# Turning the feed-forward input before it is normalised, half by half

## The chip, the cores and the metric

One core of a Trainium2 chip runs the kernel. The metric is the device time of one execution in microseconds (us). Each of the core's engines follows its own list of instructions and waits on semaphores: TensorE (PE; its weight loads are a separate row, PEld), VectorE (DVE), ScalarE (ACT), GpSimd (POOL), and SyncE (SP), which here only issues DMAs.

## The reference

Two transformer blocks over 256 tokens of width 1024. The first mixes a gated convolution, a differential attention and a cross attention. The second mixes a stick-breaking attention and a recurrent unit, adds the result to the residual, and ends with a product-key expert layer, which is where the change lies:

```python
x = x + jnp.einsum('bse,ed->bsd', mixed, w_out[l])
h = rms_norm_2(x, norm_ffn[l])          # x * rsqrt(mean(x^2) + eps) * g
# peer_ffn(h):
q = jnp.einsum('td,dhk->thk', xc, w_query)          # 8 heads x 2 sides x 128
s = jnp.einsum('thpk,hpnk->thpn', q, sub_keys)      # 128 keys per side
top_s, top_i = lax.top_k(s, PEER_TOPK)              # 16 of each side, then 16 of 256 sums
act = jax.nn.gelu(jnp.einsum('td,thkd->thk', xc, u))
return jnp.einsum('thk,thkd->td', (g * act), v)
```

For each of 256 tokens and 8 heads 16 experts are chosen out of 16384; each has a row `u` and a row `v` of 1024 numbers, which are gathered from memory.

## The kernel before

Tokens stand in two tiles of 128 (`TT` = 2), channels in eight tiles of 128 (`KT` = 8). A projection is a slot of 512 output columns; its weights come in two pieces of 256 columns. SP loads a piece into one of two raw buffers, ScalarE writes its rounded high part (L694, "hi"), VectorE the rest (L1146, "lo"), and TensorE multiplies in three products, high by high, high by low, low by high (L377). So a piece takes 48 matmuls of 256 columns, a slot 96. SP loads piece p when the low part of piece p - 2 is done; the split buffers rotate over three, so ScalarE's copy for a piece also waits for the products of the piece three back.

Each engine's order is written out by hand. Around the change it is: the sums of squares `mix1` and `mix0` (`mix_sums`, L578), ScalarE's root of them (L885), VectorE's normalisation and split of the mix (L1390 to L1403); the slots `w0` and `w1` (output projection of the second block's mix, tokens on the output partitions), VectorE adding each to the residual `x_res` (L1737, mark `x2`); then

- `inverse_rms("h3")`: squares of token tile 0 on VectorE (L1180), of tile 1 on ScalarE (L709), their sum (L1186), root (L714), reciprocal (L1190);
- `h3` = `x_res` times inverse rms times gain, on VectorE, token-major, four instructions of 512 channels (L1747). The gain `ffn_gain` is a row of 1024 on all partitions and lies in `conv_in`;
- `turn_input("h3")`: sixteen 128 x 128 transposes on TensorE (L405) into two PSUM units, then high part on ScalarE (L737) and low part on VectorE (L1213). Where a gain per channel is given, `turn_input` uses scaled forms of 256 columns (L743 and L1223), as it does for `x`, `mem` and `b2`;
- `pq0` to `pq3`, the query projections (the first piece of `pq1` is `FIRST_UNDER`); ScalarE copies the queries (L907), TensorE multiplies with the keys (`score`, L589), ScalarE copies the scores (L898).

VectorE then chooses head by head (`choose`, L1410 to L1482). Once a head of 16 picks is chosen, POOL issues 16 gathers (L1802), each 128 rows of 8 KB, `u` and `v` together; there are 256 in all, and eight row buffers. Some row buffers lie in space used earlier (`ROW_FREE`): the one in `conv_in` waits for the mark `h3`. For each pick VectorE takes the dot product of `h3` and `u` (L1489), ScalarE the gelu and a scaled identity (L923, L927), and TensorE adds the weighted `v` (L602). The projections `pq2` and `pq3` run in between.

PSUM has three units of 1024 columns and two banks of 512. `units.take` goes round the three unless a place is given; a taker waits for the previous holder's mark of release. Counting the takes, `mix1`'s sums are in unit 2, `mix0`'s in unit 0, `w0` in unit 1 and `w1` in unit 2.

Of the kernel before, what the change touches and what calls it, by code (L numbers as in the profile page):

```python
# [1 line left out]

# [3 lines left out]
P = 128  # L6
# [4 lines left out]
ACT = mybir.ActivationFunctionType  # L11
AX = mybir.AxisListType.X

T = 256
TT = T // P
D = 1024
KT = D // P
# [12 lines left out]
D_SB = SB_HEADS * SB_HEAD_DIM  # L30
D_RG = D - D_SB
RG_TILES = D_RG // P
# [13 lines left out]
           ("diff_subln_g", 1), ("x_qn_g", 2), ("x_kn_g", 2), ("norm_mix_2", KT),  # L46
           ("q_norm_2", 1), ("k_norm_2", 1), ("conv_w_2", RG_TILES * RG_WIDTH),
           ("conv_b_2", RG_TILES), ("rg_b_a_2", RG_TILES), ("rg_b_x_2", RG_TILES),
           ("rg_lambda_2", RG_TILES), ("out_norm_sb_2", D_SB // P), ("out_norm_rg_2", RG_TILES)]
VECTOR_AT = {}  # L50
for _name, _n in VECTORS:
    VECTOR_AT[_name] = (sum(n for _, n in VECTORS[:len(VECTOR_AT)]), _n)
# [3 lines left out]
class Marks:  # L56
# [13 lines left out]
    def mark(self, kind, key=None, *others, by=1):  # L70

        value = self.values[kind] = self.values.get(kind, 0) + by
        for name in (("#" + kind, value), (kind, key), *others):
            self.names[name] = kind, value
        return self.sem(kind), by
# [58 lines left out]
def build(nc, known, x, mem, vectors, w_in, w_conv_proj, w_diff_proj, w_mem_kv, w_x_proj, w_out,  # L134
          w_in_2, rg_w_a, rg_w_x, w_out_2, norm_ffn, w_query, sub_keys_t, experts, out):
    with ExitStack() as ctx:
# [214 lines left out]
        def pe(e):  # L351
# [33 lines left out]
            def project(s, between=(), place=None):  # L385
                units.take(s.name, place)
                for _ in products(s, 0):
                    pass
                for f in between:
                    f()  # L390
                for _ in products(s, 1):
                    pass

            def turn_input(pair, src, scaled, places=(None, None)):
                for half in range(2):
                    name = f"{pair} turn{half}"
                    unit = units.take(name, places[half])
                    for bank in range(2):
                        for wait in W(*(scaled(half)), units.free(name), ("ident", None)):
                            e.wait_ge(*wait)  # L400
                        for j in range(2):
                            k = 4 * half + 2 * bank + j
                            for t in range(TT):
                                to = (2 * bank + j) * T + t * P
                                m = e.transpose(unit[:, to:to + P], src[:, t, k * P:(k + 1) * P],  # L405
                                                ident[:, :])
                        m.then_inc(*mark("turned", (pair, 2 * half + bank)))

            def head_sums(name):
                sq, unit = work.ap(name), units.take(name + " sums")  # L410
# [193 lines left out]
                                 start=first, stop=g == final_pick[t])  # L604
                m.then_inc(*mark("added", g, ("uv free", g)))

            turn_input("x", x_tm, lambda half: (("scaled", "x", half, 0), ("scaled", "x", half, 1)))
            for s in slots[:4]:
                project(s)
            pending = None  # L610
            for n, s in enumerate(attention):
                if s.name == "v0":
                    turn_input("mem", mem_tm,
                               lambda half: (("scaled", "mem", half, 0), ("scaled", "mem", half, 1)))
                project(s)
                if s.name == "m0":
                    diff_values(DIFF_HEADS - 1)
                if pending in HEAD_NORMS:
                    head_sums(pending)
                elif pending:  # L620
                    diff_norm_sums(int(pending[2:]))
                pending = s.name if s.name in HEAD_NORMS else {10: "dn0", 12: "dn1"}.get(n)
                if 0 <= n - 5 < DIFF_HEADS - 1:
                    diff_values(n - 5)
                if 0 <= n - 4 < DIFF_HEADS:
                    diff_turn(n - 4)
                if 0 <= n - 3 < DIFF_HEADS:
                    diff_scores(n - 3)
                if 0 <= n - 13 < X_HEADS:
                    cross_values(n - 13)  # L630
                if 0 <= n - 12 < X_HEADS:
                    cross_turn(n - 12)
                if 0 <= n - 11 < X_HEADS:
                    cross_scores(n - 11)
# [5 lines left out]
            for name in ("xg1", "cg0", "cg1", "dp0", "dp1", "xp0", "xp1", "cp0", "cp1", "o0", "o1"):  # L640
                project(slot[name])

            turn_input("b2", xn, lambda half: (("scaled", "b2", half, 0), ("scaled", "b2", half, 1)))
            project(slot["q2"])
            project(slot["k2"])
            head_sums("q2")
# [12 lines left out]
            mix_sums(1)  # L659
            sb_values(3)  # L660
            mix_sums(0)
            project(slot["w0"])
            project(slot["w1"])

            turn_input("h3", h3, lambda half: (("h3", half),), (0, 1))
            project(slot["pq0"], place=2)
            score(0)
            project(slot["pq1"], place=2)
# [16 lines left out]
        def act(e):  # L685
# [207 lines left out]

            def score_copies(i):
                for t in range(TT):
                    for wait in W(("side_scores", (i, t))):
                        e.wait_ge(*wait)
                    e.copy(scores[t][:, 4 * i:4 * i + 4, :],  # L898
                           banks.ap(("score", i, t))[:, :].rearrange("p (s n) -> p s n", s=4)
                           ).then_inc(*mark("side_ready", (i, t), ("bank free", ("score", i, t))))  # L900

            def queries_copy(i):
                for t in range(TT):
# [206 lines left out]
            ahead(slot["w0"])  # L1110
            ahead(slot["w1"])

            inverse_rms("h3", x_res, lambda half: ("x2", half))
            turn_input("h3")
            hi(FIRST_UNDER)
            hi(FIRST_UNDER + 1)
            queries_copy(0)
# [19 lines left out]
        def dve(e):  # L1137
# [27 lines left out]
            def ahead(s, between=(), convolve=3):  # L1165
                for part in range(PIECES):
                    lo(s.n * PIECES + part + 2)
                    convolve_some(convolve)
                    if part == 0:
                        for f in between:  # L1170
                            f()
# [26 lines left out]
                                    ALU.mult).then_inc(  # L1198
                        *mark("scaled_dve", (name, half), ("scaled", name, half, 0)))

            def turn_input(pair, gain=None):
                in_hi, in_lo = pairs.ap(pair)
                for half in range(2):
                    unit = units.ap(f"{pair} turn{half}")
                    for bank in range(2):
                        k0 = 4 * half + 2 * bank
                        free = [("unit free", f"{pair} turn{half}")] if bank else []
                        both = [("in_lo", pair, k0), ("in_lo", pair, k0 + 1)]
                        if gain is None:
                            for wait in W(("in_hi", (pair, k0))):  # L1210
                                e.wait_ge(*wait)
                            turned = unit[:, bank * 512:(bank + 1) * 512]
                            e.tensor_tensor(in_lo[:, k0:k0 + 2, :],  # L1213
                                            turned.rearrange("p (j t) -> p j t", j=2),
                                            in_hi[:, k0:k0 + 2, :].bitcast(F32),
                                            ALU.subtract).then_inc(
                                *mark("in_lo", None, *both, *free))
                        else:
                            for wait in W(("in_hi", (pair, k0 + 1)), ("loaded", "vec")):
                                e.wait_ge(*wait)  # L1220
                            for j in range(2):
                                to = (2 * bank + j) * T
                                i = e.scalar_tensor_tensor(  # L1223
                                    out=in_lo[:, k0 + j, :], in0=unit[:, to:to + T],
                                    scalar=v(gain, k0 + j), in1=in_hi[:, k0 + j, :].bitcast(F32),
                                    op0=ALU.mult, op1=ALU.subtract)
                            i.then_inc(*mark("in_lo", None, *both, *free))
# [502 lines left out]
            mix_split(0, "out_norm_sb_2")  # L1730
            for i in range(2):
                ahead(slot[f"w{i}"])
                part, unit = x_res[:, :, i * SLOT:(i + 1) * SLOT], units.ap(f"w{i}")
                for wait in W(("slot", f"w{i}")):
                    e.wait_ge(*wait)
                for t in range(TT):
                    s = e.tensor_tensor(part[:, t, :], unit[:, t * SLOT:(t + 1) * SLOT],  # L1737
                                        part[:, t, :], ALU.add)
                s.then_inc(*mark("x2", i, ("unit free", f"w{i}")))

            inverse_rms("h3", x_res, lambda half: ("x2", half))
            for half in range(2):
                c = slice(half * SLOT, (half + 1) * SLOT)
                for wait in W(("inverse", "h3"), ("ffn gain", None)):
                    e.wait_ge(*wait)
                for t in range(TT):
                    s = e.scalar_tensor_tensor(  # L1747
                        out=h3[:, t, c], in0=x_res[:, t, c], scalar=inv_rms["h3"][1][:, t:t + 1],
                        in1=ffn_gain[:, c], op0=ALU.mult, op1=ALU.mult)
                s.then_inc(*mark("h3", half))  # L1750
            turn_input("h3")
            lo(FIRST_UNDER)
            lo(FIRST_UNDER + 1)
            for _ in choose(0):
                pass
# [161 lines left out]
```

## Time and profile before

| | |
|---|---|
| median of 3 runs | 1369.13 us (1367.79 to 1369.94) |
| the profiled execution's own time | 1369.03 us |
| its span, first to last instruction | 1367.3 us |
| mean granted clock of TensorE | 0.969 of full |
| busy share PE / DVE / ACT / POOL | 85% / 71% / 42% / 42% |
| chain that ended last, by engine | PE 34%, DMA 29%, DVE 23%, issue 7%, ACT 6% |

Times in a timeline count from the start of the span. A busy share is an average over the whole span and says little on a stage; what a stage is bound by is read from its own stretch. A clock of 1.00 is 2.4 GHz for TensorE, 0.50 is 1.2 GHz. The end of a matmul is modelled, and matmuls overlap: their pace is the distance from start to start.

### The profile page before, as it was taken

Reading aid. Unit: us, or ns where it says so; the run is one execution under the profiler, and the core shown is the slowest. Engines: PE = TensorE matmul, PEld = TensorE weight load, DVE = VectorE, ACT = ScalarE, POOL = GpSimd, SP = SyncE. Lnnn points to the kernel's source line nnn. Section 1 sums busy time; section 2 is a strip of 40 time slices with the busy share of each in tenths; the row PEclk is TensorE's granted clock in tenths of the full one; section 3 lists DMA queues with packets and bytes.
Section 4 is the critical chain, followed back from the end, with each engine's and each line's share of the span. In section 5 each row is a group of like instructions: output and inputs, shape, how many; then the busy total and the mean of one; then the engine's idle time right before and its main releaser. Section 6 shows DMA issues by size and latency. Waiting matters only on the chain.

```text
span 1367.3 us, 16634 instructions
## 1 busy us (share of the span) xinstructions
PE 1159.9 (85%) x6104; PEld 826.5 (60%) x6104; DVE 970.5 (71%) x1937; ACT 568.8 (42%) x1026; POOL 569.9 (42%) x576
## 2 busy tenths in 40 slices
PE   5999899999999998985878888888887778778777
PEld 5999789899999987974873443334432223222222
DVE  4488888895577655465678877778777776777554
ACT  5476656664445435775423313333222222222221
POOL 0099999999700000000023444444444444354431
PEclk9999999999999998997999999999999999999999
DMA  6644343344536544521349999999999999999996
GB/s 221 207 137 143 105 124 124 123 155 158 182 123 216 193 162 136 181 80 43 124 173 421 423 422 426 427 425 427 426 418 426 425 415 405 423 418 426 400 426 265
DMA packets 137331, 374.43 MB, mean 274 GB/s; under 512 B 6816, under 2 KB 103072, under 8 KB 104352
## 3 DMA queue, kind: packets, MB, share of 16 engines
q0 software_dynamic: 36864, 268.45, 47.0%
q1 hardware_dynamic: 98048, 99.62, 22.4%
q10 hardware_dynamic: 2336, 5.29, 1.1%
q8 instruction: 48, 0.79, 0.2%
q14 instruction: 35, 0.29, 0.1%
HBM read 372.29 MB, written 1.05 MB: 273 GB/s over the span
## 4 chain that ended last, share of the span: by engine, by line
PE 34%; DMA 29%; DVE 23%; issue 7%; ACT 6%; POOL 0%; ACTq 0%; POOLq 0%; DVEq 0%
PE unit L377 25%; DMA row<-in_experts,big 17%; DMA big<-in_experts,big 11%; PE unit L602 6%; DVE w_lo L1146 4%; DVE conv_acc L1161 3%; DVE work L1489 2%; ACT probs L927 1%; DVE big L1413 1%; ACT w_hi L694 1%; ACT probs L794 1%; DVE probs L1289 1%; DVE big L1246 1%; DVE big L1422 1%; DVE big L1419 1%
## 5 line engine op out<-in xcount | busy, mean ns | idle before, releaser
L377 PE MATMUL unit<-in_hi,w_hi 128*128 128x256 f32 x1216 | 377.4, 310 | 8.1 <-DVE probs L1361 4.8
L377 PE MATMUL unit<-in_lo,w_hi 128*128 128x256 f32 x1216 | 347.6, 286 | 0.0
L377 PE MATMUL unit<-in_hi,w_lo 128*128 128x256 f32 x1216 | 347.3, 286 | 0.0
L1802 POOL DMA_INDIRECT row<-in_experts,big x128 | 127.6, 997 | 513.4 <-DVE big L1482 336.0
L1146 DVE TENSOR_TENSOR w_lo<-w_raw,w_hi 128x2048 fp32r<-128x2048 f32 x94 | 218.8, 2330 | 117.9 <-ACT w_hi L694 117.9
L602 PE MATMUL unit<-row,probs 128*128 128x512 f32 x512 | 252.7, 620 | 57.5 <-ACT probs L927 56.6
L927 ACT ACTIVATE probs<-ident,big 128x128 f32<-128x128 f32 x256 | 102.8, 401 | 460.4 <-DVE big L1501 460.4
L377 PEld LDWEIGHTS unit<-in_hi,w_hi 128*128 128x128 f32 x1216 | 237.0, 195 | 26.7 <-issue 20.9
L377 PEld LDWEIGHTS unit<-in_lo,w_hi 128*128 128x128 f32 x1216 | 237.1, 195 | 16.1 <-issue 16.0
L602 PE MATMUL unit<-big,probs 128*128 128x512 f32 x384 | 187.8, 623 | 62.9 <-ACT probs L927 62.8
L377 PEld LDWEIGHTS unit<-in_hi,w_lo 128*128 128x128 f32 x1216 | 236.8, 195 | 0.0
L694 ACT CAST w_hi<-w_raw 128x2048 fp32r<-128x2048 f32 x94 | 176.9, 1898 | 127.1 <-PE unit L377 75.5
L1489 DVE CUSTOM_DVE_ANT_0 work<-big,row 128x1024 f32<-128x1024 f32 x128 | 156.6, 1224 | 94.2 <-DMA row<-in_experts,big 94.0
L602 PEld LDWEIGHTS unit<-row,probs 128*128 128x128 f32 x512 | 89.9, 192 | 194.9 <-ACT probs L927 129.2
L1802 POOL DMA_INDIRECT big<-in_experts,big x96 | 111.6, 1162 | 144.9 <-PE unit L602 141.8
L602 PEld LDWEIGHTS unit<-big,probs 128*128 128x128 f32 x384 | 68.0, 193 | 166.5 <-ACT probs L927 114.2
L1794 POOL TENSOR_TENSOR conv_acc<-conv_acc,big 128x256 f32<-128x256 f32 x150 | 141.7, 945 | 12.5
L1790 POOL TENSOR_SCALAR big<-conv_in,vec 128x256 f32<-128x256 f32 x150 | 141.4, 943 | 2.9
L1489 DVE CUSTOM_DVE_ANT_0 work<-big 128x1024 f32<-128x1024 f32 x96 | 116.9, 1218 | 33.6 <-DMA big<-in_experts,big 33.5
L377 PE MATMUL unit<-w_hi,in_hi 128*128 128x256 f32 x288 | 84.3, 293 | 7.6 <-DVE in_lo L1235 3.3
L377 PE MATMUL unit<-w_hi,in_lo 128*128 128x256 f32 x288 | 82.8, 288 | 0.0
L377 PE MATMUL unit<-w_lo,in_hi 128*128 128x256 f32 x288 | 82.8, 287 | 0.0
(242 smaller groups left out, 1402.6 us busy)
## 6 DMA issues: line engine op xcount, KB each, us to landing
w_raw<-in_w_in SPq DMA_DIRECT2D x58, 1024.0 KB, 5.2
w_raw<-in_w_mem_kv SPq DMA_DIRECT2D x8, 1024.0 KB, 5.3
w_raw<-in_w_out SPq DMA_DIRECT2D x8, 1024.0 KB, 5.2
w_raw<-in_w_query SPq DMA_DIRECT2D x8, 1024.0 KB, 5.4
w_raw<-in_w_diff_proj SPq DMA_DIRECT2D x4, 1024.0 KB, 5.7
w_raw<-in_w_x_proj SPq DMA_DIRECT2D x4, 1024.0 KB, 5.1
w_raw<-in_w_conv_proj SPq DMA_DIRECT2D x4, 1024.0 KB, 5.6
big<-in_x ACTq DMA_DIRECT2D x2, 1024.0 KB, 7.5
```

The lines of the kernel that those rows point to most:

```text
L377: m = e.matmul(unit[:, to:to + 256], fixed, moving, start=start, stop=stop)
L602: m = e.matmul(unit[:, half * 512:(half + 1) * 512], diag_places[g % 12], UV.ap(g)[:, D + half * 512:D + (half + 1) * 512], start=first, s ...
L694: e.copy(split.ap(p)[0][:, :, :], w_raw[p % 2][:, :, :]).then_inc(*mark("hi", p))
L794: a = e.activation(p[:, m, c], p[:, m, c], ACT.Exp, bias=few[:, i + m:i + m + 1], accum_out=few[:, 4 + i + m:5 + i + m])
L927: e.activation(diag_places[g % 12], ident[:, :], ACT.Copy, scale=here).then_inc(*mark("diag", g))
L1146: e.tensor_tensor(lo_part[:, :, :], w_raw[p % 2][:, :, :], hi_part[:, :, :].bitcast(F32), ALU.subtract).then_inc(*mark("lo", p))
L1161: i = e.scalar_tensor_tensor(out=dst, in0=src, scalar=tap, in1=dst, op0=ALU.mult, op1=ALU.add)
L1246: i = e.scalar_tensor_tensor(out=part, in0=part, scalar=gain[:, j:j + 1], in1=work.ap(name)[:, 0:n].rearrange("p (g t) -> p g t", t=T), op ...
L1489: e.tensor_tensor_reduce(out=work.ap(("dot", g))[:, 0:D], in0=h3[:, t, :], in1=UV.ap(g)[:, 0:D], scale=1.0, scalar=0.0, op0=ALU.mult, op1= ...
L1790: e.tensor_scalar(product, src, tap, 1.0, ALU.mult, ALU.mult).then_inc(*mark("pool_product", (t, k)))
L1794: e.tensor_tensor(dst, dst, product, ALU.add).then_inc(*mark("pool_tap", None, *done))
L1802: e.indirect_dma_start(out=UV.ap(g), out_offset=None, in_=experts, in_offset=bass.IndirectOffsetOnAxis(ap=expert[t][:, n:n + 1], axis=0)). ...
```

## The change

The gain moves into the vector table `vec` (8 more columns), so that `turn_input("h3", "norm_ffn_2")` applies it per channel while splitting. What is transposed is `x_res` itself, neither scaled nor multiplied by the gain. Half 0 (channels 0 to 511) is turned between the two pieces of `w1`, half 1 after it. The inverse rms is a factor per token; it is applied where the scores are copied, with `h3`'s `inv_rms` as the scale. `h3` is still made for the dot products, but later in VectorE's order. `w0` takes unit 0, `w1` unit 1, the two turns units 2 and 0.

```diff
-            project(slot["w0"])
-            project(slot["w1"])
-
-            turn_input("h3", h3, lambda half: (("h3", half),), (0, 1))
+            project(slot["w0"], place=0)
+            project(slot["w1"], [partial(turn_half, "h3", x_res, 0, (("x2", 0),), 2)], 1)
+            turn_half("h3", x_res, 1, (("x2", 1),), 0)
             project(slot["pq0"], place=2)
...
             def score_copies(i):
                 for t in range(TT):
-                    for wait in W(("side_scores", (i, t))):
-                        e.wait_ge(*wait)
-                    e.copy(scores[t][:, 4 * i:4 * i + 4, :],
-                           banks.ap(("score", i, t))[:, :].rearrange("p (s n) -> p s n", s=4)
-                           ).then_inc(*mark("side_ready", (i, t), ("bank free", ("score", i, t))))
+                    for wait in W(("side_scores", (i, t)), ("inverse", "h3")):
+                        e.wait_ge(*wait)
+                    e.activation(scores[t][:, 4 * i:4 * i + 4, :],
+                                 banks.ap(("score", i, t))[:, :].rearrange(
+                                     "p (s n) -> p s n", s=4),
+                                 ACT.Copy, scale=inv_rms["h3"][1][:, t:t + 1]).then_inc(*mark("side_ready", (i, t), ("bank free", ("score", i, t))))
...
+            turn_input("h3", "norm_ffn_2")
             inverse_rms("h3", x_res, lambda half: ("x2", half))
-            turn_input("h3")
             hi(FIRST_UNDER)
...
             for i in range(2):
                 ahead(slot[f"w{i}"])
+                if i == 1:
+                    turn_input("h3", "norm_ffn_2", (0,))
                 part, unit = x_res[:, :, i * SLOT:(i + 1) * SLOT], units.ap(f"w{i}")
...
+            turn_input("h3", "norm_ffn_2", (1,))
             inverse_rms("h3", x_res, lambda half: ("x2", half))
+            lo(FIRST_UNDER)
             for half in range(2):
...
-                    s = e.scalar_tensor_tensor(
+                    i = e.scalar_tensor_tensor(
                         out=h3[:, t, c], in0=x_res[:, t, c], scalar=inv_rms["h3"][1][:, t:t + 1],
                         in1=ffn_gain[:, c], op0=ALU.mult, op1=ALU.mult)
-                s.then_inc(*mark("h3", half))
-            turn_input("h3")
-            lo(FIRST_UNDER)
+                i.then_inc(*mark("h3", half))
             lo(FIRST_UNDER + 1)
```

`turn_half` is the old body of TensorE's `turn_input` for one half: per bank of 512 columns a wait, four transposes and a mark.

## Rows read from the trace of the kernel before

**Rows 1.** Stretches: length, busy PE, PEld, DVE, ACT, POOL (count), clock, DMA, GB/s.
```profile
708.00:760.00 52.00, 37.02 (x105) 17.82 (x106) 42.21 (x127) 16.77 (x46) 22.57 (x23) 0.90 1.01 413
...
1000.00:1340.00 340.00, 266.76 (x558) 97.31 (x559) 243.27 (x680) 89.69 (x302) 146.63 (x136) 0.98 1.01 419
```

**Rows 2.** Chain of waits in order of time: start, length, what.
```profile
651.94 20.43 PE unit L377 x168
...
677.20 3.68 PE unit L405 x16
680.88 12.23 PE unit L377 x96
```

**Rows 3.** Timeline of POOL: start, length, what, idle before and releaser.
```profile
705.92 1.15 POOL L1802 DMA_INDIRECT row<-in_experts,big  x1 [336.00 <-DVE big L1482]
```

**Rows 4.** Timeline of VectorE from the sums with the residual to the first choice.
```profile
660.88 1.29 DVE L1737 TENSOR_TENSOR big<-unit,big 128x512 f32<-128x512 f32 x2 [1.48 <-PE unit L377]
...
668.62 2.29 DVE L1146 TENSOR_TENSOR w_lo<-w_raw,w_hi 128x2048 fp32r<-128x2048 f32 x1 [2.87 <-ACT w_hi L694]
672.39 1.29 DVE L1737 TENSOR_TENSOR big<-unit,big 128x512 f32<-128x512 f32 x2 [1.48 <-PE unit L377]
...
675.73 2.74 DVE L1747 SCALAR_TENSOR_TENSOR big<-big,col,conv_in 128x512 f32<-128x512 f32 x4
...
695.58 0.29 DVE L1410 MAX8 big<-big 128x8 f32<-128x128 f32 x1 [3.93 <-ACT big L898]
```

**Rows 5.** Timeline of ScalarE in the same stretch.
```profile
666.69 1.90 ACT L694 CAST w_hi<-w_raw 128x2048 fp32r<-128x2048 f32 x1 [3.26 <-PE unit L377]
...
693.13 1.07 ACT L907 COPY work<-unit 128x512 f32<-128x512 f32 x2 [3.80 <-PE unit L377]
```

**Rows 6.** Timelines of TensorE, ScalarE and VectorE at the turn of `b2`.
```profile
527.46 3.65 PE L405 MATMUL unit<-ident,big 128*128 128x128 f32 x16 [4.75 <-DVE big L1197]
...
528.59 3.40 ACT L743 ACTIVATE in_hi<-unit,vec 128x256 fp32r<-128x256 f32 x8 [0.61 <-PE unit L405]
...
529.46 3.44 DVE L1223 SCALAR_TENSOR_TENSOR in_lo<-unit,vec,in_hi 128x256 fp32r<-128x256 f32 x8 [1.94 <-ACT in_hi L743]
```

**Rows 7.** Timeline of TensorE at the turn of `mem`.
```profile
91.23 1.91 PE L405 MATMUL unit<-ident,big 128*128 128x128 f32 x16
```

**Rows 8.** Timelines of TensorE at the start of `w0` and of ScalarE.
```profile
646.98 0.78 PE L377 MATMUL unit<-w_hi,in_hi 128*128 128x256 f32 x1
...
647.77 0.41 PE L377 MATMUL unit<-w_lo,in_hi 128*128 128x256 f32 x1
647.98 0.40 PE L377 MATMUL unit<-w_hi,in_hi 128*128 128x256 f32 x1
...
647.58 0.47 ACT L885 ACTIVATE work<-unit,col 128x256 f32<-128x256 f32 x1 [3.87 <-PE unit L578]
```

**Rows 9.** Timeline of TensorE in the second block's first projections.
```profile
545.00 0.39 PE L377 MATMUL unit<-in_hi,w_hi 128*128 128x256 f32 x1 [1.87 <-DVE w_lo L1146]
```

**Rows 10.** Stretches around idle times of TensorE, columns as in rows 1.
```profile
93.10:94.40 1.30, 0.06 (x2) 0.05 (x1) 1.30 (x3) 1.27 (x3) 1.22 (x2) 1.00 0.45 159
...
531.10:532.00 0.90, 0.90 (x7) 0.90 (x6) 0.90 (x3) 0.87 (x3) 0.00 (x0) 0.50 0.00 0
532.00:533.00 1.00, 1.00 (x9) 1.00 (x9) 0.90 (x3) 0.00 (x0) 0.00 (x0) 0.91 0.00 0
...
545.80:549.00 3.20, 3.20 (x17) 3.20 (x16) 1.35 (x1) 0.00 (x0) 0.00 (x0) 0.50 0.87 284
...
629.70:631.30 1.60, 0.00 (x0) 0.00 (x0) 0.74 (x3) 0.82 (x1) 0.00 (x0) 1.00 0.00 0
...
648.20:650.80 2.60, 2.56 (x21) 2.36 (x20) 2.56 (x4) 0.41 (x2) 0.00 (x0) 0.99 0.00 0
...
675.60:676.60 1.00, 0.00 (x0) 0.00 (x0) 0.96 (x3) 0.00 (x0) 0.00 (x0) 0.50 0.03 9
682.20:682.60 0.40, 0.40 (x4) 0.40 (x4) 0.02 (x1) 0.40 (x1) 0.00 (x0) 0.80 0.00 0
```

More of the change, by code:

```diff
@@ L1 @@
 from contextlib import ExitStack
+from functools import partial
 import concourse.bass as bass
@@ L48 @@
            ("conv_b_2", RG_TILES), ("rg_b_a_2", RG_TILES), ("rg_b_x_2", RG_TILES),
-           ("rg_lambda_2", RG_TILES), ("out_norm_sb_2", D_SB // P), ("out_norm_rg_2", RG_TILES)]
+           ("rg_lambda_2", RG_TILES), ("out_norm_sb_2", D_SB // P), ("out_norm_rg_2", RG_TILES),
+           ("norm_ffn_2", KT)]
 VECTOR_AT = {}
@@ L392, in project, with turn_half, turn_input @@
                     pass
-            def turn_input(pair, src, scaled, places=(None, None)):
-                for half in range(2):
[L396 to L399, printed above, removed]
-                            e.wait_ge(*wait)
[L401 to L407, printed above, removed]
+            def turn_half(pair, src, half, ready, place=None):
+                name = f"{pair} turn{half}"
+                unit = units.take(name, place)
+                for bank in range(2):
+                    for wait in W(*ready, units.free(name), ("ident", None)):
+                        e.wait_ge(*wait)
+                    for j in range(2):
+                        k = 4 * half + 2 * bank + j
+                        for t in range(TT):
+                            to = (2 * bank + j) * T + t * P
+                            m = e.transpose(unit[:, to:to + P], src[:, t, k * P:(k + 1) * P],
+                                            ident[:, :])
+                    m.then_inc(*mark("turned", (pair, 2 * half + bank)))
+            def turn_input(pair, src):
+                for half in range(2):
+                    turn_half(pair, src, half, (("scaled", pair, half, 0),
+                                                ("scaled", pair, half, 1)))
             def head_sums(name):
@@ L605, in add_value @@
                 m.then_inc(*mark("added", g, ("uv free", g)))
-            turn_input("x", x_tm, lambda half: (("scaled", "x", half, 0), ("scaled", "x", half, 1)))
+            turn_input("x", x_tm)
             for s in slots[:4]:
@@ L612, in pe @@
                 if s.name == "v0":
-                    turn_input("mem", mem_tm,
-                               lambda half: (("scaled", "mem", half, 0), ("scaled", "mem", half, 1)))
+                    turn_input("mem", mem_tm)
                 project(s)
@@ L641, in pe @@
                 project(slot[name])
-            turn_input("b2", xn, lambda half: (("scaled", "b2", half, 0), ("scaled", "b2", half, 1)))
+            turn_input("b2", xn)
             project(slot["q2"])
@@ L1199, in scale_tokens, with turn_input @@
                         *mark("scaled_dve", (name, half), ("scaled", name, half, 0)))
-            def turn_input(pair, gain=None):
+            def turn_input(pair, gain=None, halves=range(2)):
                 in_hi, in_lo = pairs.ap(pair)
-                for half in range(2):
+                for half in halves:
                     unit = units.ap(f"{pair} turn{half}")
```

## The prediction

> **What bounds the kernel now.** I read three views in this order. The table by stretches shows the last half: from 708 us to the end of the gathers the DMA share is 1.01 in every stretch and the rate 413 to 419 GB/s [rows 1]. So 256 gathers of 1 MB pass through a full DMA, no engine is full there, and this half ends when it started plus a fixed length. The chain of waits then says what sets its start. Reading it back from the first gather at 705.92 [rows 3], there is one serial string: `w0` and `w1` on TensorE, a gap, sixteen transposes, `pq0`, then the first scores, and from 695.58 VectorE choosing the first head [rows 2]. The timelines of VectorE and ScalarE show what the gap is made of [rows 4, 5]: `w1` ends at 672.4; the sum with the residual takes 1.29; the mean square, root and reciprocal last until 675.73; the scaled `h3` takes two instructions of 0.69 for its first half; only then, at 677.20, can a transpose start. In the gap TensorE's clock also goes to its lower level: 0.50 (1.2 GHz) from 675.6, and full (2.4 GHz) again within 682.2 to 682.6 [rows 10]. Since the gathers are bound by DMA and nothing but this string holds their start, a microsecond taken out of it should come off the end in full.
>
> **Paces used.** At full clock the 168 matmuls of the chain took 20.43, so 0.122 each [rows 2]; at half clock their starts are 0.21 apart (647.77, 647.98) [rows 8]. Sixteen transposes took 3.68 at half clock, 0.23 each [rows 2], and 1.91 at full clock, 0.12 each with the tail of the last, or 0.11 start to start [rows 7].
>
> **The change, part by part.** I count from 672.39, the end of `w1` before, to 693.13, where ScalarE takes the queries of `pq0` [rows 4, 5]: 20.74 us before.
>
> (1) Half 0 is turned between the two parts of `w1`. Its input, the first half of the sum, was ready at 662.2 [rows 4], long before the 666.7 at which part 0 ends (it released ScalarE's split of weights there [rows 5]). TensorE pays eight transposes: +0.9 at full clock (bounds 0.87, no tail, and 1.84, half clock). ScalarE then has four scaled copies and VectorE four subtractions, 0.43 each, from the eight in 3.40 and 3.44 of the turn for the second block, which has the same form with a gain [rows 6]. ScalarE starts them at 668.6, behind its weight split of 1.90; VectorE at 670.9, behind its own of 2.29, and ends at 672.6, while `w1` now ends at 673.3: 0.7 to spare. Were that gone, the delay would be the excess alone.
> (2) The sum of half 1, unchanged: 1.29, then 0.1 to TensorE.
> (3) Eight transposes of half 1 at full clock: 0.9 in place of sixteen.
> (4) `pq0` no longer waits for the split of all: it has k 0 to 3 in hand, 12 matmuls or 1.46. From the first transpose, k 4 and 5 are ready after 0.7 (four transposes and their tail; ScalarE began 1.13 behind the first at half clock [rows 6]), 0.87 (two copies ahead of VectorE, 528.59 to 529.46), 0.86 (two subtractions) and 0.1: 2.5, against 0.9 + 1.46 = 2.36 when TensorE wants them. k 6 and 7 come 0.86 later against 0.73 of work. Both stalls together: 0.3 (bounds 0 and 0.9, were the four copies finished before VectorE starts).
> (5) The 96 matmuls of `pq0` at full clock: 96 x 0.122 = 11.7, with a last tail of 0.2, 11.9. Before, the chain gives them 12.23 [rows 2], some nine of them at half clock, until 682.3.
> The sum: 0.9 + 1.4 + 0.9 + 0.3 + 11.9 = 15.4 against 20.74, so 5.3 less. With 12.23 less nine times 0.09 for the slow ones, (5) is 11.4 and the gain 5.8. I take the middle, 5.6.
> (6) The score copies become scaled activations, and only the first is on the path. Plain copies of 512 columns take 1.07 for two [rows 5]; scaled ones stand in the trace for 256 columns, 0.43 each [rows 6], so 512 lie between the plain 0.54 and 0.86. Bounds 0 and +0.3; I take 0.1, nearer to the plain copy, which reads as many columns from the same memory in one instruction.
> (7) What moves behind. ScalarE and VectorE now find the inverse rms after the split: 2.1 us (673.6 to 675.7 before), from 678.0 to 680.2, and the score copies, which newly wait for it, come at about 689. VectorE then has the weights' low part (2.29), the four `h3` instructions (2.74) and the second low part (2.29). The first waits for ScalarE's copy until 682.0, so they end at 684.3, 687.0 and 689.3; the choice of head 0 is due at 695.58 - 5.5 = 690.1. Cover of 0.8 us. It is the next thing to become late: were VectorE 1 us behind, 0.2 would show. `pq1` needs its first low part at about 690 and has it at 684.3. ScalarE's second copy of weights waits for the first part of `pq0` (near 682) and is done by 684, long before the queries. The dot products and the row in `conv_in` that wait for `h3` come over 10 us later.
> (8) Units. `w0` is put in unit 0, which the sums of `mix0` hold until ScalarE's root. That root ends at 648.05, while `w0` began at 646.98 [rows 8]. So `w0` starts 1.2 later. It then has 24 matmuls (192 of both slots less the 168) before it waits anyway until 651.94 [rows 2]. At full clock they end at 648.2 + 2.9 = 651.1: hidden, by 0.8. All at half clock they end at 653.3: +1.3. The clock was full by 648.2 before [rows 10], and I take 0. The other places have long been free.
> (9) Eight more gain columns in the first load, and no DMA moved: under 0.1, taken as 0. SP's loads are released by VectorE's low parts, the last two of which come 1 to 2 us earlier, with 10 us to spare before the gathers.
> Total: -5.6 + 0.1 = **-5.5 us**. The profiled execution took 1369.03 (span 1367.3 and 1.7 around it), 0.1 under the median of 1369.13, so 1363.6.
>
> **The clock.** TensorE's idle is now 1.4 us, then 0.9 of transposes. The profile has idles of 1.6 (629.7 to 631.3) and 1.24 (93.1 to 94.4) through which the clock stayed at 1.00 [rows 10], and one of 1.87 before 545.00 [rows 9], after which it was 0.50 from 545.8 to 549 [rows 10]. 1.4 lies on the safe side, but not far from the edge. The idle at 93.1 came right after sixteen transposes [rows 7], so for 3 us TensorE ran no other matmul and the clock held.
> The Trainium skill speaks against this (TensorE: Matmul & The Clock Gate, Part 4: PE-mode transpose): it says that transposes don't count as activity for the clock. By that rule the 1.4 and the 0.9 add up to 2.3 us without activity, longer than the idle before 545.00, and the time would be that of the first rival; the trace disagrees at 93 us, as told. After a longer idle the clock also came back with transposes: 0.50 from 531.1 to 532.0 and 0.91 in the next microsecond [rows 10], when only some 1.5 us of other matmuls stood behind the sixteen transposes from 527.46 [rows 6], while at 545 it took 4 us of matmuls.
>
> **Rivals.**
> - **The clock falls in the new gap.** For: the edge at 1.87 is near, and the gap before did it. Price: at 545.8 the lower level lasted 3.2, in the old gap 5.1 from the first transpose; half of it is lost in matmul time, 1.6 to 2.5, less the stalls of (4), which vanish. Time: -5.5 + 2.0, 1365.6.
> - **`w0` starts late and slow.** For: unit 0 is held until 648.05 and the pause falls into the time before the clock rises. Against: it rose at 648.2 when over 4 us of work had begun, of which the pause takes 1. Price 1.3: 1364.9.
> - **The gain is not passed on**, because the gathers' stretch is not rigid after all, or because the change's cover (7) is gone by more than estimated. Against: DMA share 1.01 from the first gathers. Time: some 1368.5, within 0.2%.
> - **Slower: the pause at 647 to 648 keeps TensorE at half clock on into `w1`.** The late start and 24 slow matmuls cost 1.4, every further one 0.09. The gain of 5.5 is used up at the 69th; through `w0` and half of `w1` (144) it is 12.2 lost: 1375.8. Against: at none of the places above did the lower level last longer than some 5 us once work had begun.
>
> **How the numbers follow.** Forecast 0.62 (1362.3 to 1364.8, by the bounds of (4), (5), (6) and the cover of (7)); clock falls 0.14; `w0` late 0.08; not passed on 0.12; slower 0.04. The range of 8 in 10 runs from 1361.9 to 1367.0: it takes in the first three and part of the fourth, and the 1 us by which single executions differ. Under 0.2% (2.7 us, about what a measurement of this kernel tells from no change) lie the fourth and a small part of the clock's: faster 0.83, same 0.13, slower 0.04.
>
> **What would show it.** In the changed profile: eight transposes inside `w1` at full pace; TensorE idle for about 1.4 and the clock at 1.00 through it; `pq0` starting some 2.3 us after `w1` ends with two stalls of 0.1 to 0.2; VectorE's first choice near 690; the first gather near 700.4 and the same length from there to the end. Wrong would be: 0.50 in the gap; `w0`'s wait at 651.9 later; a wait of the first choice for VectorE's own low part; or a gather stretch longer than 661.4 (705.92 to 1367.3).

## The result and the profile after

The changed kernel takes 1373.6 us (median of 7 runs, 1372.99 to 1375.22) against 1369.13 (7 runs): a ratio of 1.0037, 95% interval 1.0026 to 1.0049. It is slower by some 5 us, where 5.5 us less were forecast. Its profiled execution took 1375.07, with a span of 1373.3.

The stretch that the prediction worked out did get shorter. The chain of waits of the changed kernel (start, length, what; its rows called issue are left out: 0.61 us ahead of 649.28, 0.02 to 0.04 everywhere else):

```profile
649.28 19.23 PE unit L379 x144
668.50 0.88 PE unit L406 x8
669.38 5.77 PE unit L379 x48
675.17 1.30 DVE big L1744 x2
676.51 1.09 PE unit L406 x8
677.61 11.82 PE unit L379 x96
689.45 0.59 ACT work L912
690.09 1.17 PE bank L595 x8
691.28 0.69 ACT big L902
692.00 0.31 DVE big L1415
```

Eight transposes now stand inside `w1` (668.50, 0.88), eight behind it (676.51). From the end of `w1` (675.17) to the copy of the queries (689.45) it takes 14.28, where it took 20.74 [rows 4, 5]. With the 0.88 inside `w1` that is 5.6 less, the number that the sum had taken.

POOL's timeline, first gather of the changed kernel:

```profile
702.35 1.15 POOL L1809 DMA_INDIRECT row<-in_experts,big  x1 [331.09 <-DVE big L1487]
```

It comes 3.6 us sooner than before [rows 3], although this execution had reached the sums of `mix0` 1.1 us later (644.88 against 643.76). But from there to the end of the span it now takes 1373.3 - 702.35 = 671.0 us; before it took 1367.3 - 705.92 = 661.4. The stretch that was to be rigid is 9.6 us longer. The table by stretches (length, busy time of PE, PEld, DVE, ACT and POOL, clock, DMA share, GB/s), changed kernel:

```profile
760.00:1000.00 240.00, 199.63 (x557) 92.89 (x555) 182.26 (x507) 73.12 (x219) 106.09 (x93) 0.99 1.01 418
1000.00:1340.00 340.00, 262.29 (x551) 95.04 (x551) 240.64 (x676) 89.08 (x298) 143.06 (x134) 0.99 1.01 414
```

and the first of these stretches in the kernel before:

```profile
760.00:1000.00 240.00, 200.99 (x564) 94.02 (x562) 185.23 (x518) 73.60 (x222) 108.16 (x95) 0.99 1.01 424
```

The DMA is full in both (1.01), no engine is fuller than before, and the rate has gone from 424 to 418 GB/s, and from 419 to 414 in the long stretch [rows 1]. The DMAs move the same bytes, 374.44 MB after and 374.43 before by the page, and take about 1.4% more time for them. That points to slower transfers, and not to a wait or to another engine that holds the gathers. The experiments test this.

### The profile page after: what moved, and what is told of

Its sections match the earlier page's. It is cut to its first block, busy times and chain, and to the rows that moved or that the text cites. A ratio compares the mean times of both kernels' runs of the same rounds, so it can differ in the third digit from the quotient of the medians.

```text
span 1373.3 us, 16641 instructions
## 1 busy us (share of the span) xinstructions
PE 1162.0 (85%) x6104; PEld 825.3 (60%) x6104; DVE 972.1 (71%) x1941; ACT 570.4 (42%) x1030; POOL 568.0 (41%) x576
## 2 busy tenths in 40 slices
DMA packets 137331, 374.44 MB, mean 273 GB/s; under 512 B 6816, under 2 KB 103072, under 8 KB 104352
## 4 chain that ended last, share of the span: by engine, by line
PE 36%; DMA 28%; DVE 22%; issue 7%; ACT 6%; POOL 0%; ACTq 0%; POOLq 0%; DVEq 0%
PE unit L379 27%; DMA row<-in_experts,big 17%; DMA big<-in_experts,big 10%; PE unit L608 6%; DVE w_lo L1151 4%; DVE work L1494 3%; DVE conv_acc L1166 2%; DVE big L1418 1%; ACT probs L932 1%; ACT w_hi L698 1%; DVE big L1427 1%; ACT probs L798 1%; DVE big L1251 1%; DVE big L1424 1%; DVE big L1506 1%
## 5 line engine op out<-in xcount | busy, mean ns | idle before, releaser
L1494 DVE CUSTOM_DVE_ANT_0 work<-big,row 128x1024 f32<-128x1024 f32 x128 | 156.7, 1225 | 101.1 <-DMA row<-in_experts,big 101.1
L1797 POOL TENSOR_SCALAR big<-conv_in,vec 128x256 f32<-128x256 f32 x150 | 137.7, 918 | 2.9
```

The costliest lines, as they stand in the source:

```text
L1494: e.tensor_tensor_reduce(out=work.ap(("dot", g))[:, 0:D], in0=h3[:, t, :], in1=UV.ap(g)[:, 0:D], scale=1.0, scalar=0.0, op0=ALU.mult, op1= ...
L1797: e.tensor_scalar(product, src, tap, 1.0, ALU.mult, ALU.mult).then_inc(*mark("pool_product", (t, k)))
```

## The experiments

The change touches no gather. But it adds eight columns to the table `vec`, 32 bytes on each partition, and `vec` lies ahead of nearly all other tiles in SBUF. The programs' allocations say where the eight row buffers of the gathers start (address on the partition, and its remainder by 256; a gather writes 8192 bytes to each partition):

```
kernel            conv_in         big0, big1, big2      row0 to row3
before            35328    0      52672 ...   192       194560 ...   0
changed           35360   32      52704 ...   224       194592 ...  32
```

Of the 256 gathers 32 go to `conv_in`, 96 to `big0` to `big2` and 128 to `row0` to `row3`. The two weight buffers `w_raw` lie ahead of `vec`, at 16512 and 24704, both 128 off a multiple of 256. They are the same in every kernel here, so the weight loads play no part in the comparison, and what an aligned start would do for them was not tried.

Theory A: the DMA's destination address makes the gathers slower. Theory B: something that the change does in that stretch does (the scaled copies of scores, an earlier start against other work). The two are told apart by moving the tiles without the change, and by making the change without moving them. All kernels below were timed five times or more, each beside the kernel before; ratios are to that, with 95% intervals. Microseconds for the gather stretch and the string ahead of it come from one profiled execution of each kernel.

### The address alone

```diff
         vec = sb("vec", [VECTOR_COLS])
+        sb("pad", [8])
```

> The kernel before with an unused tile of 8 columns behind the vector table, so that every tile behind it starts 32 bytes further on, as the change makes it; nothing else. Theory A (the address): the changed kernel gathers at 420 GB/s instead of 426 in the windows from 800 us on, and from the first gather to the end it takes 671.0 us instead of 661.4, because its row buffers start 32 bytes off a multiple of 64. Then this kernel is as slow there: the gather stretch near 671, the time about 1369.1 + 9.6 = 1378.7. Theory B (the work): the stretch is longer because of what the change does in it, the scaled score copies or the earlier start against the work of the other engines. Then this kernel takes 1369.1.

Measured: 1378.47 us, ratio 1.0073 (1.0060 to 1.0087), about 10 us. The table by stretches of this kernel:

```profile
760.00:1000.00 240.00, 199.25 (x556) 92.75 (x557) 182.09 (x510) 73.43 (x221) 107.07 (x94) 0.99 1.01 418
1000.00:1340.00 340.00, 267.50 (x551) 98.30 (x549) 241.29 (x676) 88.40 (x296) 145.44 (x133) 0.96 1.01 412
```

418 GB/s, as in the changed kernel, with the same instructions as before and only the addresses moved. From the first gather (703.23) to the end of the span (1373.9) it takes 670.7, against 671.0 in the changed kernel. Theory B, as a cause of the 9.6 us, falls.

### The change with the addresses back on a multiple of 64

The same line of padding in the changed kernel; `conv_in` and the rows then start at 64 by 256, the three in `big` at 0.

> The changed kernel with an unused tile of 8 columns, so that the tiles behind the vector table lie 64 bytes further on than before the change, again on multiples of 64. Theory A: the gather stretch is 661.4 again and the gain of the first gather (702.35 against 705.92, with a start that was 1.1 us later) comes through: 1369.1 - 4.7 = 1364.4. Theory B: no change, 1373.6.

Measured: 1366.71 us, ratio 0.9991 (0.9982 to 1.0001). That is 6 to 7 us below the changed kernel, but 3 us short of what theory A gave. From the first gather (699.95) to the end of the span (1365.4) it took 665.5: between 661.4 and 671.0. So a multiple of 64 isn't the whole of it.

### The units

```diff
-            project(slot["w0"], place=0)
-            project(slot["w1"], [partial(turn_half, "h3", x_res, 0, (("x2", 0),), 2)], 1)
-            turn_half("h3", x_res, 1, (("x2", 1),), 0)
+            project(slot["w0"], place=1)
+            project(slot["w1"], [partial(turn_half, "h3", x_res, 0, (("x2", 0),), 0)], 2)
+            turn_half("h3", x_res, 1, (("x2", 1),), 1)
```

> The changed kernel with w0 in unit 1, w1 in unit 2 and the two turns in units 0 and 1, as the ring gave them before; addresses as in the changed kernel. If holding w0 back until the root of mix0 costs what the trace shows (w0 starts at once in the kernel before, and 0.6 us behind the sums in the changed one, with its first matmuls at the lower clock), from the sums of mix0 to the end of w1 it takes 29.5 instead of 30.3 us: 1372.8. If the wait was hidden, 1373.6.

Measured: 1372.38 us, ratio 1.0029 (1.0018 to 1.0040) against 1.0037. The times alone can't part the two. The traces can: from the first of `mix0`'s sums to VectorE's addition of `w1` it takes 29.28 here (644.55 to 673.83) and 30.29 in the changed kernel (644.88 to 675.17). TensorE's timeline in the changed kernel (start, length, what, idle before and releaser):

```profile
644.88 3.78 PE L584 MATMUL unit<-work,ones 128*128 128x256 f32 x8 [4.80 <-ACT work L885]
649.28 0.55 PE L379 MATMUL unit<-w_hi,in_hi 128*128 128x256 f32 x1 [0.61 <-issue]
...
652.62 0.41 PE L379 MATMUL unit<-w_hi,in_hi 128*128 128x256 f32 x1
652.83 0.41 PE L379 MATMUL unit<-w_hi,in_lo 128*128 128x256 f32 x1
```

and with the old units:

```profile
644.55 3.58 PE L584 MATMUL unit<-work,ones 128*128 128x256 f32 x8 [4.37 <-ACT work L885]
647.77 0.48 PE L379 MATMUL unit<-w_hi,in_hi 128*128 128x256 f32 x1
...
648.32 0.28 PE L379 MATMUL unit<-w_hi,in_hi 128*128 128x256 f32 x1
648.44 0.28 PE L379 MATMUL unit<-w_hi,in_lo 128*128 128x256 f32 x1
```

`w0` starts 4.4 us after the sums instead of 3.2, and its matmuls still come 0.21 apart at 652.8 (half clock), 8 us after work began, while with the old units they are 0.12 apart from 648.1 on. VectorE has the first tile of `mix0`'s split ready near 653 in the changed kernel, and TensorE is then still at its first 24 matmuls: in this execution the wait was not hidden, and it cost 1.0 us.

It is not so in every execution. Two other kernels keep the units of the changed one, with the same pause of 0.61 us: after_shift64, above, and after_align, further below. In after_shift64 it again takes 30.25 (642.54 to 672.79), and the matmuls come 0.12 apart only from 8.2 us after the sums began. In after_align they do so from 4.4 us on (the pause ends at 648.08), and from the sums to the addition of `w1` it takes 29.30 (643.87 to 673.17), no more than with the old units. Its chain of waits:

```profile
643.87 3.61 PE unit L587 x8
...
647.51 0.48 ACT work L892
...
651.86 14.65 PE unit L382 x120
```

Here, as in the kernel before, TensorE waits for the split until 651.86, and the pause is hidden, which is what step (8) had forecast. So the pause costs some 1 us when the clock rises late, which two of the three kept traces show, and nothing when it rises early.

> Both edits on the changed kernel. Theory A with the units: 1369.1 - 5.5 = 1363.6. Theory B with the units: 1372.8.

Measured: 1365.69 us, ratio 0.9987 (0.9979 to 0.9996), again with 665.3 from the first gather (697.44) to the end (1362.7).

### Which remainder counts

128 bytes of padding behind `vec` in the kernel before:

> The kernel before with every tile behind the vector table 128 bytes further on: all eight row buffers then start on a multiple of 64, none on a multiple of 256 (rows and the one in conv_in at 128, the three in big at 64). In the kernel before five of eight start on a multiple of 256 (conv_in and the four of row) and three at 192. From the first to the last gather's issue it took 638.2 us before, 646.8 in the changed kernel (none on a multiple of 256), 641.5 in after_shift64 (three of eight). Theory A256: what counts is the multiple of 256, and each of the 256 gathers into another address costs 0.053 us: 96, 256 and 160 of them fit these three. Then this one takes 638.2 + 160 x 0.053 = 646.7, time 1367.8 + 8.6 = 1376.4. Theory A64: what counts is the multiple of 64 (the page of the Trainium skill on DMA speaks of 256, but 32-byte beats are its unit). Then it takes 638 to 641 and 1368 to 1371.

Measured: 1374.59 us, ratio 1.0049 (1.0036 to 1.0062); 668.1 from first gather to end (704.38 to 1372.5). All starts are multiples of 64 and of 32, and still it is 6 to 7 us slower. A multiple of 64 is not enough. But it is less than the 10 us of 32 bytes (the two intervals just touch), so one cost for every gather that isn't on a multiple of 256 looks too simple as well.

All eight on a multiple of 256, in the kernel before:

```diff
         conv_in = sb("conv_in", [KT, CONV_K - 1 + T])
+        sb("pad_a", [16])
...
         col = sb("col", [128])
+        sb("pad_b", [48])
```

> The kernel before with unused tiles of 64 bytes behind conv_in and 192 behind the small tiles, so that all eight row buffers start on a multiple of 256. Theory A256: the 96 gathers that were off a multiple win 0.053 each: from first to last gather 633.1, time 1367.8 - 5.1 = 1362.7. Theory A64: no change, 1367.8.

Measured: 1365.24 us, ratio 0.9980 (0.9971 to 0.9988): 2.7 us faster than the kernel before, by padding alone; 659.1 from first gather to end (704.59 to 1363.7). Its table by stretches:

```profile
760.00:1000.00 240.00, 200.22 (x565) 93.35 (x563) 185.09 (x520) 74.32 (x225) 105.00 (x96) 1.00 1.01 426
1000.00:1340.00 340.00, 268.44 (x560) 98.52 (x560) 243.87 (x678) 89.50 (x302) 146.14 (x136) 0.98 1.01 421
```

The direction is A256's and excludes A64; the size is half of the 5.1 expected.

### What the change is worth with the addresses out of it

The changed kernel with 224 bytes behind `vec` and the two pads above, so that all eight start on a multiple of 256:

> The changed kernel with all eight row buffers on multiples of 256. This takes the address out of the comparison, so against before_align it shows what the change itself is worth: 4.7 us by the first gathers of the two traces. Theory A256: 1362.7 - 4.7 = 1358.0. Theory A64: 1367.8 - 4.7 = 1363.1. If the change costs something in the gather stretch besides the address: over 1360 against a before_align of 1362.7.

Measured: 1362.46 us, ratio 0.9953 (0.9940 to 0.9966). That is above the 1358.0 of theory A256, but before_align is above its 1362.7 as well, so the pair has to be compared. Against before_align the ratio is 0.9953 / 0.9980 = 0.9973, 3.7 us; the expectation was 4.7, and the intervals together leave some 2 us of room. The other pair with equal remainders, the changed kernel and before_shift32, gives 1.0037 / 1.0073 = 0.9964, 4.9 us.

> The same with w0, w1 and the turns in the units of the kernel before (w0 doesn't wait for the root of mix0). Theory A256: 1357.2; A64: 1362.3. Against after_align the units are worth 0.8 by the trace, about as much as this measurement can tell.

Measured: 1360.27 us, ratio 0.9936 (0.9923 to 0.9949), 8.8 us faster than the kernel before, and 6.0 faster than before_align by the ratios (0.9956). The times put it 2.2 us below after_align. The intervals just overlap, and the two traces show no gain from the units (29.48 from the sums to the addition of `w1` against 29.30). It is the fastest kernel measured here, and the version to keep.

### Whose address

In before_align, row0 to row3 32 bytes further on (pad_b of 56 columns):

> before_align with the four buffers row0 to row3, and the small splits beside them, 32 bytes further on; the other four row buffers stay on multiples of 256. Half of the gathers then land 32 bytes off. If the cost goes gather by gather with its own destination: from 256 gathers off (before_shift32, 0.9% over before_align) half of it, 6 us: 1365.2 + 6 = 1371.5. If any misplaced tile slows all: as before_shift32, 1377.

Measured: 1369.82 us, ratio 1.0014 (1.0005 to 1.0023), 4.7 us over before_align, and 663.8 from first gather to end (704.65 to 1368.4) against 659.1. All eight off cost 12.7 us (1.0073 against 0.9980). Half of the gathers cost somewhat less than half of that, and far less than all of it, so it goes by the gather and not by a worst case.

In before_align, only the tiles from `work` to `col` 32 bytes further on (besides those that the expectation names also `probs_t`, `ones64`, `later`, `before` and `iota16`):

> before_align with the tiles work, probs, ident, ones, dist and col 32 bytes further on, and all eight row buffers kept on multiples of 256. These tiles are read and written by engines all through the gather stretch, and no gather goes there. If the DMA's destination is what counts: as before_align, 1365.2. If it is the engines' operands: up to 1377.

Measured: 1364.05 us, ratio 0.9976 (0.9962 to 0.9990), as before_align. The address of these operands doesn't matter.

One rival is left by this, for a row buffer is not only written by a gather: VectorE and TensorE read it, so moving it moves an operand of theirs too. The pages settle that. VectorE's dot product with `row` in before_align, and in before_shift32, where every buffer is misplaced:

```profile
L1491 DVE CUSTOM_DVE_ANT_0 work<-big,row 128x1024 f32<-128x1024 f32 x128 | 156.7, 1225 | 94.6 <-DMA row<-in_experts,big 94.6
...
L1490 DVE CUSTOM_DVE_ANT_0 work<-big,row 128x1024 f32<-128x1024 f32 x128 | 156.7, 1224 | 101.8 <-DMA row<-in_experts,big 101.8
```

One takes 1225 ns in the first and 1224 in the second; what grows is VectorE's wait for the DMA, 94.6 to 101.8 us. TensorE's matmuls with `row` average 618 and 623 ns, with an engine that is idle for part of the stretch. So it is the DMA's destination that counts.

256 bytes behind `vec` in the kernel before:

> The kernel before with all tiles behind the vector table 256 bytes further on. Each start keeps its remainder by 256. If only the remainder counts: 1368.5, as before. If it is the distance itself or a fuller memory: slower, by up to the 10 us of 32 bytes.

Measured: 1367.62 us, ratio 0.9998 (0.9989 to 1.0007). The distance moved is nothing by itself; the remainder is.

Put together, by the traces' time from the first gather to the end of the span:

```
gathers off a multiple of 256    kernel, us
  0                              align_small32 658.6, before_align 659.1, after_align_units 659.9, after_align 660.4,
                                 late_half (below) 660.5
 96 at 192                       before_shift256 660.9, before 661.4
128 at 32                        align_rows32 663.8
160 at 64                        after_shift64_units 665.3, after_shift64 665.5
160 at 128, 96 at 64             before_shift128 668.1
160 at 32, 96 at 224             before_shift32 670.7, changed 671.0, after_units 671.8
```

In the first line the three kernels with the change lie 0.8 to 1.9 us above the two without it. That may be a small cost of the change in the gathers' stretch, or the spread of single executions; no run here tells.

### The half inside `w1`

after_align_units with both halves turned behind `w1`:

```diff
-            project(slot["w1"], [partial(turn_half, "h3", x_res, 0, (("x2", 0),), 0)], 2)
+            project(slot["w1"], place=2)
+            turn_half("h3", x_res, 0, (("x2", 1),), 0)
             turn_half("h3", x_res, 1, (("x2", 1),), 1)
```

(with ScalarE's and VectorE's part of half 0 moved along).

> after_align_units with both halves turned behind w1 (unscaled, gain in the split, inverse rms in the score copies, as there). It parts the gain: what is left is that of the scaling taken off the path; what is missing is that of the half turned inside w1. pq0 then waits for the first split, 2.5 us behind the first transpose, and meets three stalls of 0.13, against 0.9 + 0.9 + 0.3: 0.8 us over after_align_units, 1361.1. If TensorE's clock falls in the gap (1.4 idle, 1.8 of transposes, 0.8 idle), 2 more: 1363.

Measured: 1362.05 us, ratio 0.9958 (0.9944 to 0.9972). From VectorE's addition of `w1` to the queries it takes 15.85 (669.52 to 685.37) against 14.28 + 0.88 in after_align_units: 0.7 more, as expected, and the clock stayed at 1.00 from 670 to 684. By the traces, then, nearly all of the gain of the string, some 5 of 5.6 us, is from taking the mean square, the root and the scaling off the path, and turning half a slot early is worth 0.7. The times don't settle this share: they differ by 0.22%, 3 us, with intervals that just overlap, and against before_align they give 3.0 us to late_half and 6.0 to after_align_units. They say that the late half isn't faster, and leave room for anything from a few tenths to over 5 us.

## Why the prediction was wrong, point by point

- **What bounds the kernel: right in kind, wrong in one word.** The gathers do fill the DMA, and nothing but the string ahead of them sets their start. But "this half ends when it started plus a fixed length" made a rate of this layout into a constant. Between 760 and 1000 us it is 424 GB/s in the kernel before (the prediction's "413 to 419" leaves this stretch out), 417 to 418 with the buffers at 32 and 224, and 423 to 426 with all on multiples of 256. The sign that it had named for being wrong, a gather stretch longer than 661.4, is the one that came: 671.0.
- **The step that failed is (9).** It counted the eight columns as a longer first load, "under 0.1, taken as 0", and not as 32 bytes in front of everything. "No DMA moved" holds for the order of the DMAs, but each of the 256 gathers now lands 32 bytes further on. This term measured 10 us in before_shift32 (ratio 1.0073), against the 5 us that the rest of the change wins: 10 - 5 = 5, which is the measured 1.0037. The rival "the gain is not passed on" named the gathers' stretch, but as something that would swallow the gain, with no mechanism that could go beyond it. The rival on the slower side was another.
- **The sum (1) to (5): right.** 15.16 measured (14.28 and 0.88) against 15.4 from the paces, 14.9 with the chain's own for (5), and 15.1 as taken. Term by term: the addition and the step to TensorE 1.34 (675.17 to 676.51) against 1.4; eight transposes 0.85 against 0.9. The stalls came to 0.1 to 0.2 against 0.3.
- **(6): right.** The scaled score copy took 0.69, the plain one in the kernel before 0.59; +0.1.
- **(7): right.** VectorE's second low part ended at 690.5 and the first choice began at 692.0, released by the score copy.
- **(8): wrong in the profiled execution.** The rival "`w0` starts late and slow" came true beside everything else: 1.0 us, of a price of 1.3. The step took the old clock's rise at 648.2 for granted. But the pause lies ahead of the rise, and in this execution, as in that of after_shift64, the rise came only after most of the first 24 matmuls, near 653. In after_align it came 4.4 us after the sums began, and the wait was hidden as forecast; so the step was right or wrong by when the clock rose. The slower rival, that the lower level might last on into `w1`, did not happen.
- **The clock in the new gap: right.** TensorE's stretches in the changed kernel, idle and then transposes:

```profile
675.20:676.50 1.30, 0.00 (x0) 0.00 (x0) 1.26 (x2) 0.00 (x0) 0.00 (x0) 1.00 1.07 382
676.50:677.60 1.10, 1.09 (x10) 1.09 (x11) 0.00 (x0) 0.39 (x2) 0.00 (x0) 1.00 0.92 314
677.60:680.00 2.40, 2.40 (x20) 2.21 (x19) 1.92 (x5) 2.40 (x8) 0.00 (x0) 1.00 0.01 2
```

  The clock is 1.00 through 1.3 us of idle and the transposes behind it. The same stretch, from the addition of `w1` to the queries, took 14.27 or 14.28 us in all six kept traces with a half turned inside `w1`, so the clock held in each. In late_half, with 1.3 of idle, sixteen transposes and another 0.6 of waiting for the first split, it held as well. The rule of the Trainium skill that speaks against it (TensorE: Matmul & The Clock Gate, Part 4: PE-mode transpose), that a transpose doesn't count as busy time for the clock in the same way, is not borne out by any of these.

With its own terms and only (9) and (8) mended, the sum comes to 1369.1 - 5.5 + 1.0 + 10 = 1374.6, against 1373.6. Both mended terms are measured and not forecast.

## What to carry to other kernels

- A tile that grows moves every tile behind it. Where a stretch is bound by DMA, write down where its destinations start before and after the change, modulo 256, and put small or growing tables behind the large buffers, or pad them. Here that was worth more than the change itself, and padding the old kernel alone gave 2.7 us.
- To time a change of code, hold the addresses fixed: a kernel with only the move, and one with only the code, part the two at once.
- A taker of a buffer that is late by 1 us is not safely hidden by a later wait. Where the pause falls ahead of the clock's rise, the work between can run at half pace too: it did in two of three traces here. One trace shows what happened once, so read a second before pricing such a pause.

## What the runs showed of the hardware

A gather that writes 8192 bytes to each of 128 partitions takes longer where its SBUF destination doesn't start on a multiple of 256 bytes. By the ratios over before_align, and the number of gathers that are off: 10 + 2.7 us by 256 is 0.050 us for each at 32 and 224; 9.4 by 256 is 0.037 at 128 and 64; 4.7 by 128 is 0.037 at 32 (its intervals leave some 0.03 to 0.05); 2.7 by 96 is 0.028 at 192. A gather takes about 2.5 us of a full DMA (659 us for 256, with their end), so this is 1 to 2%. Whether each remainder has its own price, as the first two suggest, the intervals don't quite settle. The addresses of the engines' tiles made no difference (0.9976 against 0.9980), and neither did a shift of everything by 256 (0.9998).

The Trainium skill has a possible reason (DMA: Bandwidth & Descriptors, How a descriptor splits into AXI transactions): when a descriptor does not start on a multiple of 256 bytes, its first bus transaction starts at the boundary below, and the bytes ahead of the start cost as well. For 8192 bytes that would be 33 transactions in place of 32, an estimate of 3% from that page, or, in the page's beats of 32 bytes, 1 more in 256 at a remainder of 32 and 7 more at 224, an estimate of 0.4 to 2.7%. Measured are 1 to 2%. By beats 192 should cost more than 32; measured are 0.028 and 0.037, the other way round, though the intervals are wide. The page says this of reading, the runs show a cost for the side written. The mechanism itself is argued and not shown: no run here looks inside a transfer.

TensorE's clock stayed at 0.50 until near 653 in the changed kernel, 8 us after work had begun at 644.88, with one pause of 0.6 us in it. That is longer than any lower level that the prediction had found. In the eleven kept traces without the pause, matmuls at the pace of the full clock began 3.5 to 5.1 us after the sums began; in the three with it, 8.4, 8.2 and 4.4 us after. So a pause can go with a much later rise, but need not.
